# First weight transfer split, two small loads moved to ScalarE, two warm-up products fewer, in a hybrid decoder layer step

## The reference

```python
def _rmsnorm(x, g):
    xf = x.astype(jnp.float32)
    y = xf * lax.rsqrt(jnp.mean(xf * xf, axis=-1, keepdims=True) + EPS)
    return (y * g.astype(jnp.float32)).astype(x.dtype)
...
    proj = h @ w_in
    cv, cg, q, f, v, og, ga, gb = jnp.split(proj, _split_offsets(), axis=-1)
```

## Time and profile before

| what | us |
|---|---|
| median of 3 timed executions | 810.92 (810.8 to 811.32) |
| the profiled execution, device time | 811.34 |
| its span (first to last instruction of the trace) | 809.4 |
| PE busy | 776.1 (96% of the span) |
| DVE, ACT, POOL busy | 232.8, 176.6, 96.3 |
| DMA | 268.16 MB, mean 331 GB/s |

### The profile page before, as it was taken

How to read it: one execution, slowest core, us unless ns; L and a number is a source line. 1 busy time by engine, 2 the same in 40 slices (tenths; PEclk the granted TensorE clock), 3 DMA queues, 4 the chain that set the end, 5 groups by cost and what they waited for, 6 DMA issues and landing times.

```text
span 809.4 us, 10141 instructions
## 1 busy us (share of the span) xinstructions
PE 776.1 (96%) x4170; PEld 450.4 (56%) x4170; DVE 232.8 (29%) x533; ACT 176.6 (22%) x321; POOL 96.3 (12%) x127
## 2 busy tenths in 40 slices
PE   8999999999999999999999999999998998999996
PEld 7888887888888888853333333333322333344331
DVE  4099869381551222431110111011101101101112
ACT  3104433558445001321111101100110010011001
POOL 5200064524200000001101000001000000000001
PEclk9999999999999999999999999999999999999999
DMA  9844586578849963589999999999999999999993
GB/s 327 243 166 171 165 259 197 154 229 180 281 149 389 402 249 138 210 326 430 421 430 395 423 428 426 427 428 425 428 424 428 428 425 428 423 430 419 421 420 115
DMA packets 75607, 268.16 MB, mean 331 GB/s; under 512 B 5791, under 2 KB 37771, under 8 KB 58784
## 3 DMA queue, kind: packets, MB, share of 16 engines
q1 hardware_dynamic: 73570, 264.13, 83.7%
q0 software_dynamic: 528, 1.90, 0.6%
q10 hardware_dynamic: 1461, 1.45, 0.6%
HBM read 259.40 MB, written 8.55 MB: 331 GB/s over the span
## 4 chain that ended last, share of the span: by engine, by line
PE 78%; DMA 16%; DVE 2%; issue 1%; ACT 1%; POOL 1%; SPq 0%; DVEq 0%
PE bank L1603 23%; PE bank L1980 22%; PE bank L2018 10%; DMA slots<-in_w_expert_gate_dram 10%; PE bank L1876 7%; PE bank L2027 5%; DMA slots<-in_w_expert_up_dram 5%; PE bank L1823 2%; PE bank L1713 1%; PE bank L2007 1%; DVE early L1461 1%; DMA slots<-in_w_in_dram 1%; PE bank L1944 1%; PE bank L1635 1%; ACT wrep L1026 1%
## 5 line engine op out<-in xcount | busy, mean ns | idle before, releaser
L1603 PE MATMUL bank<-hT,slots 128*128 128x264 f32 x832 | 189.6, 387 | 0.0
L1980 PE MATMUL bank<-slots,hT 128*64 128x512 f32 x624 | 178.4, 595 | 5.5 <-DMA slots<-in_w_expert_gate_dram 4.9
L1603 PEld LDWEIGHTS bank<-hT,slots 128*128 128x128 f32 x832 | 156.6, 190 | 26.8 <-issue 0.6
L1461 DVE TENSOR_TENSOR early<-early,bank 128x512 f32<-128x512 f32 x16 | 11.0, 688 | 382.1 <-PE bank L1980 382.1
L1980 PEld LDWEIGHTS bank<-slots,hT 128*64 128x64 f32 x624 | 55.2, 137 | 99.4 <-issue 89.2
L2018 PE MATMUL bank<-slots,wrep 128*64 128x512 f32 x304 | 86.4, 595 | 4.2 <-ACT wrep L1026 4.1
L1980 PE MATMUL bank<-slot,hT 128*64 128x512 f32 x208 | 83.0, 594 | 2.1 <-DMA slot<-in_w_expert_gate_dram 2.1
L766 POOL COPY hT<-early 128x512 f32 x30 | 17.5, 612 | 373.9 <-PE bank L1980 290.4
L2027 PE MATMUL bank<-hT,diag 128*128 128x512 f32 x128 | 59.2, 605 | 0.2 <-ACT hT L1038 0.2
L2018 PEld LDWEIGHTS bank<-slots,wrep 128*64 128x64 f32 x304 | 28.3, 137 | 44.4 <-issue 35.4
L1201 DVE SCALAR_TENSOR_TENSOR slot<-slot,rows_buf 128x256 f32<-128x256 f32 x120 | 49.4, 488 | 0.0
(11 more groups left out here) (313 smaller groups left out, 813.6 us busy)
## 6 DMA issues: line engine op xcount, KB each, us to landing
slots<-in_w_expert_down_dram SPq DMA_DIRECT2D x17, 2048.0 KB, 32.6
slots<-in_w_expert_gate_dram SPq DMA_DIRECT2D x15, 2048.0 KB, 27.2
slots<-in_w_expert_up_dram SPq DMA_DIRECT2D x15, 2048.0 KB, 32.2
slots<-in_w_in_dram SPq DMA_DIRECT2D x13, 2048.0 KB, 10.3
slots<-in_w_expert_gate_dram SPq DMA_DIRECT2D x10, 1024.0 KB, 26.7
slot<-in_w_expert_gate_dram SPq DMA_DIRECT2D x5, 2048.0 KB, 31.7
slot<-in_w_expert_up_dram SPq DMA_DIRECT2D x5, 2048.0 KB, 27.7
slot<-in_w_expert_down_dram SPq DMA_DIRECT2D x5, 2048.0 KB, 36.9
```

The lines of the kernel that those rows point to most:

```text
L1461: dve.tensor_tensor(act.rearrange("s (f c) -> s f c", f=FT), act.rearrange("s (f c) -> s f c", f=FT), bank[UP][:, :].rearrange("s (c f) -> ...
L1603: last = mm(out, w[:, a, t * P:(t + 1) * P], (hT if c else xgain)[:, a, :], start=(a == 0), stop=(a == KT - 1))
L1980: last = mm(out[sl, :], xe[:, a, sl], expert_view(p, kind, e, a // 4)[:, a % 4, :], start=(a == 0), stop=(a == KT - 1))
```

## The change

The norm weight and the sample rows of x are issued by ScalarE, as its first two instructions in the program's text, so SyncE begins with the two prompt tiles of x. The leading half of the first weight chunk is loaded in two transfers: blocks 0 and 1 (512 KB, `first_in`), and blocks 2 and 3 (512 KB, a new semaphore `second_in`). TensorE waits for `second_in` ahead of a = 2. After the sample rows' transposes two warm-up products are run in place of four.

```diff
         def _(sp):
-            xp, xs = ins["x_prompt"][0], ins["x_sample"].rearrange("b t d -> (b t) d")
-            sp.dma_start(vecr[0:KT, :], ins["norm_mix_g"][0].rearrange("(r c) -> r c", c=P)).then_inc(gain_in, 16)
-            sp.dma_start(xtok[0:NB, 2, :], xs).then_inc(x_in[2], 16)
+            xp = ins["x_prompt"][0]
             for i in range(2):
                 sp.dma_start(xtok[:, i, :], xp[i * P:(i + 1) * P, :]).then_inc(x_in[i], 16)
...
-            sp.dma_start(slot3(0)[:, 0:KT // 2, :], stream[0][0][:, 0:KT // 2, :]).then_inc(first_in, 16)
+            sp.dma_start(slot3(0)[:, 0:2, :], stream[0][0][:, 0:2, :]).then_inc(first_in, 16)
+            sp.dma_start(slot3(0)[:, 2:KT // 2, :], stream[0][0][:, 2:KT // 2, :]).then_inc(second_in, 16)
             sp.dma_start(slot3(0)[:, KT // 2:, :], stream[0][0][:, KT // 2:, :]).then_inc(stream_in[0], 16)
...
+            se.dma_start(vecr[0:KT, :], ins["norm_mix_g"][0].rearrange("(r c) -> r c", c=P)).then_inc(gain_in, 16)
+            se.dma_start(xtok[0:NB, 2, :], ins["x_sample"].rearrange("b t d -> (b t) d")).then_inc(x_in[2], 16)
             for i in (2, 0, 1):
                 m = TOK_TILES[i][1]
                 se.wait_ge(x_in[i], 16)
...
             last.then_inc(x_turned, 1)
-            keep_busy(4)
+            keep_busy(2)
             pe.wait_ge(x_in[0], 16)
...
                 for a in range(4 * half, 4 * half + 4):
+                    if a == 2:
+                        pe.wait_ge(second_in, 16)
                     pe.wait_ge(x_gained, a + 2)
```

More of the change, by code:

```diff
@@ L274, in hybrid_layer @@
         x_turned, x_gained, x_copied = sem("x_turned"), sem("x_gained"), sem("x_copied")
-        first_in, gain_in = sem("first_in"), sem("gain_in")
+        first_in, second_in, gain_in = sem("first_in"), sem("second_in"), sem("gain_in")
         x_squared, rms_ready, diag_ready = sem("x_squared"), sem("rms_ready"), sem("diag_ready")
```

## The result

The changed kernel takes 812.55 us (median of 13 executions, 811.22 to 813.51) against 810.83 us (809.25 to 811.46) for the kernel before on the same chips: ratio 1.0021, 95% interval 1.0013 to 1.0029. It is 1.7 us slower, where 1.2 us faster was forecast, and above the range's end of 811.9. The profiled execution took 812.48 us, its span is 810.5.

What follows compares the result with a forecast made beforehand. PE was taken to bound the kernel (78% of the chain), its start held by the first weights' transfer. Starting 1.36 us sooner turns 811.34 into 809.98, and the median's 0.42 less gives 809.6 us; range 808.5 to 811.9.

Steps and rivals of the forecast that it cites:

- the sample rows on ScalarE's queue: At the start, rows sharing engines with x's first tile: delay bounded by 0 and 1.9 us, taken 0 to 0.3, entered 0.
- The rule on turns: Transfer engines alternate between queues by packet, so the small rows are not stuck behind x's 512 KB; no delay added.
- the sum: Whole program: 1.36 us off the profiled execution's 811.34 gives 809.98, less 0.42 to the median, hence 809.6.
- rival C: At the start, ScalarE's table load precedes its issues; rows land at 4.4, total 811.5 to 813.0, say 812.0; chance 0.12.
- the table load: ScalarE's 1.28 us load at the start: expected behind its issues, 1.6 to 2.9, hidden before the sample rows land.
- the main line: The forecast itself: first products start 1.36 us sooner and this reaches the end, 809.6 us; chance 0.60.
- the halving near 7.2 us: PE's instruction spacing at the start falls from 0.21 to 0.11 us near 7.2, so x's transposes end at 8.1.
- Two products fewer save 0.85 us: PE's warm-ups: two fewer let x's transposes start at 5.15 in place of 6.00.
- The taps: Their transfer on ScalarE's queue, in by 23.2 against use at 23.56; a gain above about 1.8 us would meet it.
- x and the weights: SyncE's landings at the start: x tiles at 4.6 and 5.9 us, weight parts at 7.35 and 8.64.
- `second_in` cost nothing: PE's added wait ahead of a = 2: needed at 10.0 us, there at 8.64, so no cost.
- a moved start does go on to the end: Expert-stage transfers hang on PE's progress, so a shift of PE's start at 9.46 moves all the rest.

Runs made afterwards that it cites:

- e8: Changed kernel with SyncE waiting for the norm weight's landing before issuing the second x tile; its one execution took 812.94 us.
- e14: Second profiled execution of the unchanged kernel before; no ratio given, first products at 9.89 us.
- e10: Kernel before with only the taps issued ahead of the eight vectors, in two transfers; ratio 1.0003 to before.
- e6: Kernel before with only the leading half of the weights split in two transfers; ratio 0.9995 to before.
- e12: e9 with four warm-up products in place of two; ratio 0.9987 to before.
- e1: Changed kernel with norm weight and sample rows issued by SyncE again, split and two warm-ups kept; ratio 0.9995 to before.
- e7: Kernel before with only two warm-up products in place of four; ratio 0.9998 to before.
- e5: Changed kernel with sample rows back as SyncE's first issue, only the norm weight on ScalarE; ratio 0.9993 to before.
- e9: e5 with the taps issued ahead of the eight vectors, in two transfers; ratio 0.9993 to before.
- e4: Changed kernel with four more warm-up products ahead of the wait for the sample rows; ratio 1.0010 to before.
- e16: Changed kernel with PE turning the first prompt tile ahead of the sample rows, three warm-ups before it, ScalarE squaring in that order; ratio 0.9992 to before.
- e17: e16 with the taps issued ahead of the eight vectors, in two transfers; ratio 0.9992 to before.
- e2: Kernel before with only the norm weight and sample rows moved to ScalarE; ratio 1.0023 to before.
- e3: Changed kernel with ScalarE's two issues exchanged, sample rows first; ratio 1.0009 to before.
- e11: Changed kernel with the taps issued ahead of the eight vectors, in two transfers; ratio 1.0009 to before.
- e13: Changed kernel with both edits of e4 and e11: four more warm-ups and the earlier, two-part taps issue; ratio 1.0009 to before.
- e15: Second profiled execution of the changed kernel; no ratio given, first products at 11.04 us.

## Why the prediction was wrong

- **The step that failed** is the sample rows on ScalarE's queue: "I take 0 to 0.3 ... I enter 0". The bounds were 0 and 1.9, and it came to 1.9: 3.77 us from issue to landing against 1.9 before. I took the lower end because of a share of "one packet or two". The row that the upper bound came from, x's own 3.8 us, was the right one, since the rows came in behind much of x (e8). Against the forecast the transposes of x start 2.05 us late (7.20 for 5.15), which is the rows, and the first products another 0.47 (10.62 for 8.1), which is PE's pace.
- **The rule on turns was read wrongly.** The Trainium skill, DMA: Bandwidth & Descriptors (Queues, rings and completion order), says that each engine takes turns between its queues, a packet at a time, and I let the sum stay by it. But a packet there is about 9 to 17 descriptors, while the profile's packets here are single rows of 4 KB and signals (55 of them, 0.21 MB). A 512 KB tile is 128 rows, 8 for each of the 16 engines. If a row is one descriptor, an estimate from the page's figure is that one turn can take a tile's whole share of an engine. So the rule never promised the rows soon after 3.3, and their 3.33 us with one tile ahead (e8) do not contradict it; no run here shows the turns themselves.
- **The mechanism of rival C was right in its place and wrong in its cause.** It said that the rows decide if they land after 4.2, and gave a start at 10.0 and 811.5 to 813.0. Measured: 5.2, 10.62, 812.55. But it hung on the table load, which ran behind the issues as the main line had it, and so got 0.12. I had priced the delay there and not on the queue, where it also belonged.
- **PE's pace.** The forecast took the halving near 7.2 us, from one execution. Where PE has four warm-ups and no idle, the 16 transposes lasted 2.49, 3.34, 2.77, 3.25 and 3.26 us (before, e14, e10, e6, e12); with two warm-ups 3.67, 3.67, 3.63 and 3.51 (e1, e7, e5, e9); with idle 3.62 in all but e4. The execution of before that I worked from was the quickest of the five. "Two products fewer save 0.85 us" is right for the start (5.24 for 6.00) and wrong for the end of the transposes, start plus length: on the mean 8.86 in e1, e5, e7 and e9 against 9.00 in the five with four. Of 0.85 us, 0.15 is left.
- **The taps** were named as the next wait, at a gain of more than 1.8 us. They bit in e6, at a start only 0.4 us sooner: the landing of one execution (before 24) does not hold for another (25.3).
- **Right:** x and the weights landed within 0.1 us of the numbers; `second_in` cost nothing; ScalarE's table load ran behind its issues; and a moved start does go on to the end. By the medians it does so one for one, as forecast (1.65 us at the taps, 1.72 in the time); the two profiled pairs have 1.2 us left of it at 776, within what two executions of one kernel differ by.

## What to carry to other kernels

In this kernel a small transfer was on time when it was issued ahead of the large ones or together with the first: the rows took 1.9 us as SyncE's second issue, and ScalarE's first issue at most 2.5. As ScalarE's second issue, with a megabyte issued by SyncE a moment before, it took 3.65 to 4.50. So the shorter issue list of one engine can be paid with the wait of another, and the thing to look at is what is already under way, not only which queue is free. (A small transfer behind x on SyncE's own queue was not tried.) If it must be late, let the engine do first what does not need it (e16). When a start is brought forward, look up each later transfer that has no wait now; here one that was in time in one execution held PE for 0.9 us in the next version's. And a warm-up that is cut because the engine "only waits" may be doing its work: on the mean two fewer brought the start of the transposes 0.75 us forward, and their end 0.15.

## What the runs showed of the hardware

- Of two small transfers issued by ScalarE at 0.81 and 1.43, while SyncE issued 512 KB at 0.81 and again near 1.25, the first was in at most 2.5 us after its issue (2.41 in e16 and e17, where PE waited for it) and the second took 3.65 to 4.50 us (after, e2, e3, e4, e11, e13, e15), 4 KB as much as 32 KB. With the second 512 KB held back it took 3.33 (e8).
- PE's 128x128 instructions follow one another at 0.21 us at first and at 0.11 later, as between 1.2 and 2.4 GHz; the change came at 7.2 us in before and not by 11.6 in e17, while the granted clock shows 1.00 in both. By the length of the transposes it came later where PE had idled or had fewer warm-up products before it.
- The one-piece transfer of 31 rows of 2 KB took 10.6 to 11.4 us from issue to landing where PE waited for it (after, e2, e3, e4, e6, e8, e15, e16), beside the weight stream. Issued ahead of the eight vectors as 16 and 15 rows, the two took 4.7 to 5.5 us each (e9 to e13, e17).
- At the routing the granted clock was 0.50 in some executions and 1.00 in others of the same kernel, and the stretch took 1.0 to 1.2 us longer at 0.50.
